# Second mixer: six weight units and the step widths computed from unscaled rows, their outputs multiplied by the token norm's root

## The chip, the core and the metric

One core of a Trainium2 chip runs the whole kernel. Its engines are TensorE (PE, with its weight loads shown apart as PEld), VectorE (DVE), ScalarE (ACT), GpSimd (POOL) and SyncE (SP), which issues the transfers. Each engine takes its own instructions in order, and they meet through semaphores. The metric is device time in microseconds (us) of one execution.

## The reference

The program is two transformer blocks over 256 tokens of width 1024. The first block (a mixer and a mixture of experts, ending in a layer norm) leaves `h`, 256 x 1024. The second block begins with the part that is changed:

```python
u = rmsnorm(h, norm_mix_w)            # h * rsqrt(mean(h*h) + EPS) * w, one root for each token
proj = u @ w_in                       # 1024 x 10272
gate_a, gate_s, b_a, c_a, v_a, z, xbc, dt_raw = split(proj)
y_a = (b_a * causal_dwconv(c_a * v_a)) @ w_a_out
...                                   # scan over xbc with the step widths softplus(dt_raw + dt_bias)
merged = sigmoid(gate_a) * y_a + sigmoid(gate_s) * y_s
h = h + merged @ w_o
```

The root belongs to a token and the sum of `u @ w_in` runs over features, so the root may be applied to the rows before the product or to the product's columns of that token behind it.

## The kernel before

Everything is fp32 in and out. A product of two fp32 matrices is made of three passes in fp32r: each operand is split into a high part (rounded by an ACT copy) and a low part (the rest, by a DVE subtract), and `product3` (L168, L169, L170) issues high x high, low x high and high x low.

The second mixer (`mixer2`) streams 56 weight units. A unit is 1024 x 256 weights (1 MB). SP loads it into one of three slots; ACT makes the high part (`split_hi`, L112, 128x2048), DVE the low part (`split_lo`, L116), and PE multiplies (`unit`, `gemm`, `features_out`: 2 x 8 x 3 matmuls of 128x256), with features on the partitions and the 256 tokens along the free dimension, into one of three banks in turn. The high part of unit n overwrites that of unit n-3, so `split_hi(n)` waits for the end of unit n-3:

```python
def split_hi(act, n):
    st.hi(act, n // 3, n % 3, KD * COLS, n - 2 if n >= 3 else None)
```

Units 0 to 11 hold b_a, c_a and v_a; their outputs are copied by ACT from the bank into `bcv` (`evac`, L1725), each copy ahead of `split_hi(n + 3)` in ACT's order. Units 12 to 23 go through a convolution. Units 0 to 2 are written out in PE's code, units 3 to 23 are a loop.

The start of the mixer runs in this order. DVE finishes the layer norm of the first block for token tile 0, then tile 1 (L228), and each adds one to `s.h_ready`. ACT computes for each tile the mean of squares and the root (L1702, L234, L236) and writes `diag`, the identity times the root (L1706). PE has six filler matmuls (L1993) in front, waits for both tiles, and turns `h` by 16 fp32 matmuls with `diag` on the moving side (L1998), so the rows in banks 3 to 6 are turned and scaled by the root at once. ACT copies them with the norm's weight into `u_hi` (L1709), DVE makes `u_lo` (L1838), and unit 0 starts, its first eight products each waiting for one `u_lo`. Behind unit 0 PE multiplies the 32 columns of the step widths (`w_dt_hi`, `w_dt_lo`), ACT copies the 32 rows out (L1712), PE turns them in two small transposes behind unit 1 (L2022), and DVE and ACT compute softplus (L1844 to L1849, L1715 to L1721).

DVE's own order at that place is `split_lo(0)`, two small operations (`half_norm_w`, `w_dt_lo`), the eight `u_lo`, `split_lo(1)`, `split_lo(2)`, the step widths, and then `split_lo(3)` to `split_lo(14)`.

Of the kernel before, what the change touches and what calls it, by code (L numbers as in the profile page):

```python
# [1552 lines left out]
def mixer2(nc, A, s):  # L1553

    XBC_TAPS, A_TAPS, N_HEADS, N_GROUPS = 4, 3, 32, 4
    with ExitStack() as ctx:
        def sb(name, shape, dt=FP32):
            return ctx.enter_context(nc.sbuf_tensor(name, shape, dt))
# [64 lines left out]
        bank_of, use_of = {}, {}  # L1623
# [71 lines left out]
        def scalar(act):  # L1695
# [1 line left out]
            split_hi(act, 1)  # L1697
            act.wait_ge(par_loaded, 48)
            act.activation(w_dt_hi[:, :, :], w_dt[:, :, :], ACT.Copy).then_inc(w_dt_split, 1)
            for t in range(TT):  # L1700
                act.wait_ge(s.h_ready, t + 1)
                own.add(act.activation(squares_of_h, s.h[:, t, :], ACT.Square, accum_out=mv[:, t, 0:1]))  # L1702
                own.wait()
                inverse_root(act, own, mv[:, t, 2:3], mv[:, t, 1:2], mv[:, t, 0:1], 1.0 / D, s.eps_ln, r_ready)
                act.wait_ge(r_ready, t + 1)
                act.activation(diag[:, t, :], C("identity"), ACT.Copy, scale=mv[:, t, 2:3]).then_inc(diag_ready, 1)  # L1706
            for k in range(KD):
                act.wait_ge(ut_mm, k // 2 + 1)
                act.activation(u_hi[:, k, :], s.bank[3 + k // 2][:, T * (k % 2):T * (k % 2) + T], ACT.Copy, scale=s.col("norm_mix_w_2", k)).then_inc(ut_hi, 1)  # L1709
            split_hi(act, 2)  # L1710
            act.wait_ge(dt_heads_mm, 1)
            act.activation(dt_heads, s.bank[7][0:N_HEADS, P:P + T], ACT.Copy).then_inc(dt_copied, 1)  # L1712
            act.preload_act_table_set(LOG_EXP)
            act.wait_ge(dt_raw, 1)
            own.add(act.activation(dt_tmp[:, :, :], dt[:, :, :], ACT.Abs))  # L1715
# [7 lines left out]
            def evac(n, dst, func, scale=1.0, signal=None):  # L1723
                act.wait_ge(st.gemm_done, n + 1)
                act.activation(dst, s.bank[bank_of[n]][:, :], func, scale=scale).then_inc(signal or evac_sem[bank_of[n]], 1)  # L1725

            for n in range(12):
                evac(n, pair(bcv, n), ACT.Copy)
                split_hi(act, n + 3)

            def ya_part(j):
                act.wait_ge(ya_ready, j + 1)
# [95 lines left out]
        def vector(dve):  # L1828
# [5 lines left out]
            dve.wait_ge(w_dt_split, 1)  # L1834
            dve.tensor_tensor(w_dt_lo[:, :, :], w_dt[:, :, :], w_dt_hi[:, :, :].bitcast(FP32), ALU.subtract).then_inc(w_dt_split, 1)
            for k in range(KD):
                dve.wait_ge(ut_hi, 2 * (k // 2) + 2)
                dve.scalar_tensor_tensor(out=u_lo[:, k, :], in0=s.bank[3 + k // 2][:, T * (k % 2):T * (k % 2) + T], scalar=s.col("norm_mix_w_2", k),  # L1838
                                         in1=u_hi[:, k, :].bitcast(FP32), op0=ALU.mult, op1=ALU.subtract).then_inc(ut_lo, 1)
            for n in range(1, 3):  # L1840
                split_lo(dve, n)
            dve.wait_ge(dt_mm, 1)
            dve.wait_ge(par_loaded, 48)
            dve.tensor_tensor(dt[:, :, :], s.bank[7][:, 0:64].rearrange("p (t h) -> p t h", t=TT),  # L1844
# [3 lines left out]
            dve.wait_ge(dt_ready, 1)  # L1848
            dve.scalar_tensor_tensor(out=loga[:, :, :], in0=dt[:, :, :], scalar=-1.0, in1=a_col[:, :].unsqueeze(1).to_broadcast([P, TT, N_HEADS]),  # L1849
                                     op0=ALU.mult, op1=ALU.mult).then_inc(dt_ready, 1)  # L1850
            for n in range(3, 15):
                split_lo(dve, n)

            def conv_a_part(j):

# [134 lines left out]
        def tensor(pe):  # L1990

            for i in range(6):
                pe.matmul(s.bank[1][:, :], lhsT=C("identity"), rhs=s.con[:, 1:5, :].rearrange("p n c -> p (n c)"), start=True, stop=True)  # L1993
            pe.wait_ge(s.h_ready, 2)
            for t in range(TT):
                pe.wait_ge(diag_ready, t + 1)
                for k in range(KD):
                    m = pe.matmul(s.bank[3 + k // 2][:, T * (k % 2) + P * t:T * (k % 2) + P * t + P], lhsT=s.h[:, t, k * P:k * P + P], rhs=diag[:, t, :], start=True, stop=True)  # L1998
                    if t == 1 and k % 2:
                        m.then_inc(ut_mm, 1)  # L2000

            def gemm(q, i, bank, x, first=True, last=True, used=None, wait_k=None):

# [5 lines left out]
            def unit(n, x, **kw):  # L2009
                gemm(n // 3, n % 3, bank_of[n], x, used=use_of[n], **kw)  # L2010

            u, ya = (u_hi, u_lo), (ya_hi, ya_lo)
            unit(0, u, wait_k=lambda k: pe.wait_ge(ut_lo, k + 1))

            pe.wait_ge(w_dt_split, 2)
            for k in range(KD):
                m = product3(pe, s.bank[7][0:N_HEADS, P:P + T], (w_dt_hi[:, k, :], w_dt_lo[:, k, :]), (u_hi[:, k, :], u_lo[:, k, :]), k == 0, k == KD - 1)
            m.then_inc(dt_heads_mm, 1)
            unit(1, u)
            pe.wait_ge(dt_copied, 1)  # L2020
# [495 lines left out]
```

## Time and profile before

| what | value |
|---|---|
| time, median of 3 runs (lowest to highest) | 1704.86 us (1702.92 to 1706.76) |
| profiled execution: time, span in the trace | 1705.02 us, 1703.2 us |
| granted TensorE clock, mean over the span | 0.995 |
| PE busy | 1655.8 us (97%) |
| DVE busy | 676.8 us (40%) |
| ACT busy | 577.0 us (34%) |
| second mixer's first unit starts, in the trace | 1146.38 us |

The span is the part of the profiled execution that the trace covers; 1.8 us lie around it. A clock of 1.00 is the full 2.4 GHz, 0.50 is 1.2 GHz. Busy matmuls overlap each other in the trace (a 128x256 matmul is shown with 0.28 us, and the next begins 0.12 us after it), so PE's progress is read from starts.

### The profile page before, as it was taken

The page shows a single profiled execution, that of the slowest core. Times are in us where ns is not written, and L with a number is a line of the kernel's source. Part 1 is how long each engine was busy: PE and PEld are TensorE (multiplying, and loading weights), DVE is VectorE, ACT ScalarE, POOL GpSimd, SP SyncE. Part 2 cuts the span into 40 slices and gives each one's busy share as a digit, 9 for nine tenths or more (in the row PEclk, how much of TensorE's full clock was granted, in tenths as well). Part 3 has the DMA queues.
Part 4 walks back from the last instruction along what each step waited for, and adds up shares of the span by engine and source line. Part 5 has one row for each costly group of instructions (what it writes and reads, how often), then busy time and mean ns, then how long its engine had stood idle before and what let it go on. Part 6 is the DMA issues. An engine that isn't in the chain of part 4 may idle for free.

```text
span 1703.2 us, 23986 instructions
## 1 busy us (share of the span) xinstructions
PE 1655.8 (97%) x9921; PEld 1053.1 (62%) x9921; DVE 676.8 (40%) x1196; ACT 577.0 (34%) x819; POOL 42.8 (3%) x28
## 2 busy tenths in 40 slices
PE   8999999989999999999999999989999999999998
PEld 8999853333333333333333333349999999989996
DVE  4676641212121211121212121244597565666654
ACT  5655321111111111110111111144464787466433
POOL 0000000000000000000000000000100032000000
PEclk9999999999999999999999999999999999999999
DMA  8556899999999999999999999975555443555552
GB/s 266 199 198 222 303 392 423 428 412 428 431 430 431 431 428 431 429 431 429 432 429 431 428 429 428 431 279 182 181 179 174 149 149 124 177 182 183 187 185 87
DMA packets 150864, 535.15 MB, mean 314 GB/s; under 512 B 7890, under 2 KB 102510, under 8 KB 118030
## 3 DMA queue, kind: packets, MB, share of 16 engines
q1 hardware_dynamic: 150798, 534.20, 79.7%
q8 instruction: 50, 0.82, 0.2%
q14 instruction: 16, 0.13, 0.0%
HBM read 533.13 MB, written 1.05 MB: 314 GB/s over the span
## 4 chain that ended last, share of the span: by engine, by line
PE 62%; DMA 12%; SPq 2%; ACT 1%; DVE 1%; issue 0%; ACTq 0%
PE bank L1434 16%; PE bank L168 10%; PE bank L170 10%; PE bank L169 10%; PE bank L1450 8%; DMA expert_weights<-in_expert_w_up_dram 6%; DMA expert_weights_late<-in_expert_w_up_dram 6%; PE bank L1395 2%; PE bank L1414 2%; PE bank L1441 2%; SPq L1642 1%; PE bank L1403 1%; PE bank L2046 0%; ACT back_w_hi L112 0%; PE bank L1408 0%
## 5 line engine op out<-in xcount | busy, mean ns | idle before, releaser
L1332 DVE TENSOR_TENSOR pre_act<-bank,bias_now 128x512 f32<-128x512 f32 x64 | 44.0, 688 | 655.3 <-PE bank L1441 655.3
L116 DVE TENSOR_TENSOR back_w_lo<-raw_weights,back_w_hi 128x2048 fp32r<-128x2048 f32 x90 | 205.7, 2288 | 91.8 <-ACT back_w_hi L112 90.8
L1434 PE MATMUL bank<-expert_weights_late,x_gathered 128*64 128x512 f32 x1024 | 226.2, 593 | 13.7 <-DMA expert_weights_late<-in_expert_w_up_dram 13.7
L112 ACT ACTIVATE back_w_hi<-raw_weights 128x2048 fp32r<-128x2048 f32 x90 | 170.2, 1892 | 95.1 <-PE bank L170 94.6
L168 PE MATMUL bank<-u_hi,back_w_hi 128*128 128x256 f32 x704 | 200.0, 284 | 0.2 <-DVE u_lo L1838 0.2
L169 PE MATMUL bank<-u_lo,back_w_hi 128*128 128x256 f32 x704 | 199.1, 283 | 0.0
L170 PE MATMUL bank<-u_hi,back_w_lo 128*128 128x256 f32 x704 | 199.1, 283 | 0.0
L1434 PE MATMUL bank<-expert_weights,x_gathered 128*64 128x512 f32 x752 | 167.0, 594 | 8.7 <-DMA expert_weights<-in_expert_w_up_dram 8.7
L1434 PEld LDWEIGHTS bank<-expert_weights_late,x_gathered 128*64 128x64 f32 x1024 | 72.3, 137 | 164.2 <-issue 136.2
L1254 ACT ACTIVATE raw_weights<-bank 128x512 f32<-128x512 f32 x32 | 19.1, 597 | 399.6 <-PE bank L1434 399.6
L168 PEld LDWEIGHTS bank<-u_hi,back_w_hi 128*128 128x128 f32 x704 | 135.0, 192 | 1.0 <-issue 0.7
L169 PEld LDWEIGHTS bank<-u_lo,back_w_hi 128*128 128x128 f32 x704 | 135.0, 192 | 0.0
L170 PEld LDWEIGHTS bank<-u_hi,back_w_lo 128*128 128x128 f32 x704 | 135.0, 192 | 0.0
L1434 PEld LDWEIGHTS bank<-expert_weights,x_gathered 128*64 128x64 f32 x752 | 53.0, 137 | 118.9 <-issue 99.7
L1450 PE MATMUL bank<-expert_weights_late,activations 128*64 128x512 f32 x512 | 113.4, 595 | 0.2 <-DVE activations L1345 0.2
L168 PE MATMUL bank<-v_hi,back_w_hi 128*128 128x256 f32 x352 | 99.9, 284 | 0.2 <-DVE v_lo L2266 0.2
L169 PE MATMUL bank<-v_lo,back_w_hi 128*128 128x256 f32 x352 | 99.6, 283 | 0.0
L170 PE MATMUL bank<-v_hi,back_w_lo 128*128 128x256 f32 x352 | 99.6, 283 | 0.0
L1270 ACT ACTIVATE raw_weights<-bank 128x512 f32<-128x512 f32 x32 | 19.1, 597 | 206.2 <-PE bank L1450 206.2
L1450 PE MATMUL bank<-expert_weights,activations 128*64 128x512 f32 x368 | 82.0, 594 | 0.0
L168 PE MATMUL bank<-x_hi,m_w_hi 128*128 128x256 f32 x272 | 78.1, 287 | 0.0
L169 PE MATMUL bank<-x_lo,m_w_hi 128*128 128x256 f32 x272 | 76.8, 282 | 0.0
(424 smaller groups left out, 2649.9 us busy)
## 6 DMA issues: line engine op xcount, KB each, us to landing
expert_weights_late<-in_expert_w_up_dram SPq DMA_DIRECT2D x64, 2048.0 KB, 25.6
expert_weights<-in_expert_w_up_dram SPq DMA_DIRECT2D x47, 2048.0 KB, 25.3
expert_weights_late<-in_expert_w_down_dram SPq DMA_DIRECT2D x32, 2048.0 KB, 29.2
raw_weights<-in_w_in_dram SPq DMA_DIRECT2D x56, 1024.0 KB, 5.3
expert_weights<-in_expert_w_down_dram SPq DMA_DIRECT2D x23, 2048.0 KB, 28.6
raw_weights<-in_expert_w_up_dram SPq DMA_DIRECT2D x15, 2048.0 KB, 23.8
raw_weights<-in_w_up_dram SPq DMA_DIRECT2D x22, 1024.0 KB, 5.1
raw_weights<-in_expert_w_down_dram SPq DMA_DIRECT2D x8, 2048.0 KB, 28.7
```

The source lines that it names most:

```text
L112: act.activation(self.w_hi[:, s, 0:size], self.s.raw[:, s, 0:size], ACT.Copy).then_inc(self.hi_done, 1)
L116: dve.tensor_tensor(self.w_lo[:, s, 0:size], self.s.raw[:, s, 0:size], self.w_hi[:, s, 0:size].bitcast(FP32), ALU.subtract).then_inc(self. ...
L168: pe.matmul(out, lhsT=ah, rhs=bh, start=start, stop=False, skip_group_check=shared)
L169: pe.matmul(out, lhsT=ah, rhs=bl, start=False, stop=False, skip_group_check=shared)
L170: return pe.matmul(out, lhsT=al, rhs=bh, start=False, stop=stop, skip_group_check=shared)
L1254: act.activation(up_rows[:, 0, :], U[0][:, :], ACT.Copy).then_inc(up_out, 1)
L1332: dve.tensor_tensor(both.rearrange("p g k n -> p (g k) n").rearrange("p a (h n) -> p a h n", h=2), TB[b][:, :].rearrange("p (a h n) -> p a ...
L1395: m = pe.matmul(TB[0][rows[c], :], lhsT=onehot[:, t, :], rhs=s.h[:, t, 512 * c:512 * c + 512], start=(t == 0), stop=(t == 1))
L1414: m = pe.matmul(s.bank[ACC + 2 * t + c][:, :], lhsT=scatter[rows[c], P * t:P * t + P], rhs=y_rows[rows[c], :], start=False, stop=True, ski ...
L1434: m = pe.matmul(U[b][rows[half], :], lhsT=xg[:, 2 * u + a, :], rhs=w[:, a, 512 * c:512 * c + 512], start=(first and a == 0), stop=(last an ...
L1441: m = pe.transpose(TB[b][:, P * gk:P * gk + P], up_rows[:, b, gk:512:4], C("identity"))
L1450: m = pe.matmul(U[0][rows[c], :], lhsT=act_t[:, b, g, half, :], rhs=w[:, half, g, 512 * c:512 * c + 512], start=(b + half + g == 0), stop= ...
```

## The change

The rows of `h` are now turned without the root, by transposes against the identity. ACT and DVE split them into `raw_u_hi` and `raw_u_lo`, and units 0 to 5 and the step widths are multiplied from these. ACT computes the root of tile 0 ahead of the raw high parts and that of tile 1 behind them. PE spreads the roots over the partitions by two matmuls of a matrix of ones with `diag` (into bank 2), ACT copies them to `root_rows`, and DVE multiplies the outputs of units 0 to 5 (`scaled_copy`, in place of ACT's copies) and the step widths by them. Meanwhile DVE makes the scaled rows `scaled_u` from the turned banks, ACT and DVE split them into `u_hi` and `u_lo`, two rows at a time among the units' own work, and from unit 6 on PE uses `u_hi` and `u_lo` as before. PE waits once for all eight `u_lo`, ahead of unit 6. Units 0 to 5 are written out, units 6 to 23 are the loop.

```diff
@@ scalar (ACT)
-            for t in range(TT):
+            def root(t):
                 act.wait_ge(s.h_ready, t + 1)
 ...
+            root(0)
             for k in range(KD):
                 act.wait_ge(ut_mm, k // 2 + 1)
-                act.activation(u_hi[:, k, :], s.bank[3 + k // 2][:, T * (k % 2):T * (k % 2) + T], ACT.Copy, scale=s.col("norm_mix_w_2", k)).then_inc(ut_hi, 1)
+                act.activation(raw_u_hi[:, k, :], turned(k), ACT.Copy, scale=s.col("norm_mix_w_2", k)).then_inc(raw_hi, 1)
+            root(1)
             split_hi(act, 2)
-            act.wait_ge(dt_heads_mm, 1)
-            act.activation(dt_heads, s.bank[7][0:N_HEADS, P:P + T], ACT.Copy).then_inc(dt_copied, 1)
+            act.wait_ge(bc_mm, 1)
+            act.activation(root_rows, s.bank[2][:, 0:T], ACT.Copy).then_inc(bc_ready, 1)
+            split_hi(act, 3)
 ...
             for n in range(12):
-                evac(n, pair(bcv, n), ACT.Copy)
-                split_hi(act, n + 3)
+                if n >= RAW_UNITS:
+                    evac(n, pair(bcv, n), ACT.Copy)
+                if n:
+                    split_hi(act, n + 3)
+                if 1 <= n < 5:
+                    for k in range(2 * n - 2, 2 * n):
+                        act.wait_ge(rescaled, k + 1)
+                        act.activation(u_hi[:, k, :], scaled_u[:, k, :], ACT.Copy).then_inc(ut_hi, 1)
@@ vector (DVE)
+            dve.wait_ge(bc_ready, 1)
+            dve.wait_ge(dt_heads_mm, 1)
+            dve.tensor_tensor(dt_heads, s.bank[7][0:N_HEADS, P:P + T], root_rows[0:N_HEADS, :], ALU.mult).then_inc(dt_copied, 1)
+
+            def scaled_copy(n):
+                dve.wait_ge(st.gemm_done, n + 1)
+                dve.tensor_tensor(bcv[:, 2 * n:2 * n + 2, :], s.bank[bank_of[n]][:, :].rearrange("p (a t) -> p a t", a=2),
+                                  root_rows.unsqueeze(1).to_broadcast([P, 2, T]), ALU.mult).then_inc(evac_sem[bank_of[n]], 1)
+
+            scaled_copy(0)
+            split_lo(dve, 3)
 ...
-            for n in range(3, 15):
-                split_lo(dve, n)
+            for n in range(1, 12):
+                if n < RAW_UNITS:
+                    scaled_copy(n)
+                if n < 3:
+                    for k in range(4 * n - 4, 4 * n):
+                        dve.scalar_tensor_tensor(out=scaled_u[:, k, :], in0=turned(k), scalar=s.col("norm_mix_w_2", k), in1=root_rows,
+                                                 op0=ALU.mult, op1=ALU.mult).then_inc(rescaled, 1)
+                split_lo(dve, n + 3)
+                if 2 <= n < 6:
+                    for k in range(2 * n - 4, 2 * n - 2):
+                        dve.wait_ge(ut_hi, k + 1)
+                        dve.tensor_tensor(u_lo[:, k, :], scaled_u[:, k, :], u_hi[:, k, :].bitcast(FP32), ALU.subtract).then_inc(ut_lo, 1)
@@ tensor (PE)
+            def turn_u(t, k):
+                return pe.transpose(turned(k)[:, P * t:P * t + P], s.h[:, t, k * P:k * P + P], C("identity"))
+
+            pe.wait_ge(s.h_ready, 1)
+            for k in range(6):
+                turn_u(0, k)
             pe.wait_ge(s.h_ready, 2)
-            for t in range(TT):
-                pe.wait_ge(diag_ready, t + 1)
-                for k in range(KD):
-                    m = pe.matmul(s.bank[3 + k // 2][:, T * (k % 2) + P * t:T * (k % 2) + P * t + P], lhsT=s.h[:, t, k * P:k * P + P], rhs=diag[:, t, :], start=True, stop=True)
-                    if t == 1 and k % 2:
-                        m.then_inc(ut_mm, 1)
+            for k in range(KD):
+                if k >= 6:
+                    turn_u(0, k)
+                m = turn_u(1, k)
+                if k % 2:
+                    m.then_inc(ut_mm, 1)
 ...
-            unit(0, u, wait_k=lambda k: pe.wait_ge(ut_lo, k + 1))
+            unit(0, raw_u, wait_k=lambda k: pe.wait_ge(raw_lo, k + 1))
 ...
+            for t in range(TT):
+                pe.wait_ge(diag_ready, t + 1)
+                m = pe.matmul(s.bank[2][:, P * t:P * t + P], lhsT=C("ones"), rhs=diag[:, t, :], start=True, stop=True)
+            m.then_inc(bc_mm, 1)
+            unit(1, raw_u)
 ...
-            unit(2, u)
-            with pe.Fori(1, 8) as q:
+            pe.wait_ge(bc_ready, 1)
+            for n in range(2, RAW_UNITS):
+                unit(n, raw_u)
+            pe.wait_ge(ut_lo, KD)
+            with pe.Fori(RAW_UNITS // 3, 8) as q:
                 for i in range(3):
                     gemm(q, i, i, u, used=q)
```

Two places in the engines' orders matter. The first is DVE between the layer norm's end and unit 12 (the `x_b_c` row is unit 12's convolution). Before, with `back_w_lo` the weights' low parts:

```order
L228 SCALAR_TENSOR_TENSOR hidden<-hidden,expert_weights_top 128x1024
L116 TENSOR_TENSOR back_w_lo<-raw_weights,back_w_hi 128x2048
L1833 TENSOR_SCALAR half_norm_w<-parameter_cols 128x16
L1835 TENSOR_TENSOR w_dt_lo<-w_dt,w_dt_hi 128x256
L1838 SCALAR_TENSOR_TENSOR u_lo<-bank,parameter_cols,u_hi 128x256 x8
L116 TENSOR_TENSOR back_w_lo<-raw_weights,back_w_hi 128x2048 x2
L1844 TENSOR_TENSOR dt<-bank,dt_bias 128x64
L1847 SCALAR_TENSOR_TENSOR dt<-dt,dt_tmp 128x64
L1849 SCALAR_TENSOR_TENSOR log_a<-dt,a_log 128x64
L116 TENSOR_TENSOR back_w_lo<-raw_weights,back_w_hi 128x2048 x12
```

The same place now, from the low part of weight unit 5 (the `b_c_v` rows are `scaled_copy`, `squares` holds `root_rows`, `gates` holds `scaled_u`, whose eight rows are made further ahead in two groups of four):

```order
L116 TENSOR_TENSOR back_w_lo<-raw_weights,back_w_hi 128x2048
L1890 TENSOR_TENSOR u_lo<-gates,u_hi 128x256 x2
L1865 TENSOR_TENSOR b_c_v<-bank,squares 128x512
L116 TENSOR_TENSOR back_w_lo<-raw_weights,back_w_hi 128x2048
L1890 TENSOR_TENSOR u_lo<-gates,u_hi 128x256 x2
L1865 TENSOR_TENSOR b_c_v<-bank,squares 128x512
L116 TENSOR_TENSOR back_w_lo<-raw_weights,back_w_hi 128x2048
L1890 TENSOR_TENSOR u_lo<-gates,u_hi 128x256 x2
L1865 TENSOR_TENSOR b_c_v<-bank,squares 128x512
L116 TENSOR_TENSOR back_w_lo<-raw_weights,back_w_hi 128x2048
L1890 TENSOR_TENSOR u_lo<-gates,u_hi 128x256 x2
```

The four L116 rows are the low parts of units 5, 6, 7 and 8, and the three L1865 rows between them multiply the outputs of units 3, 4 and 5. So the low part of a weight unit now stands between each two pairs of `u_lo`, and that of unit 8 ahead of the last pair.

The second place is ACT's order from the layer norm's end to the step widths (L112 is the high part of a weight unit). Before, with L1702 to L1706 the root of a tile:

```order
L1702 ACTIVATE z,rms_mv<-hidden 128x1024
L234 ACTIVATE rms_mv<-rms_mv,eps 128x1
L236 ACTIVATE rms_mv<-rms_mv 128x1
L1706 ACTIVATE group_rstd<-shared_constants,rms_mv 128x128
L1702 ACTIVATE z,rms_mv<-hidden 128x1024
L234 ACTIVATE rms_mv<-rms_mv,eps 128x1
L236 ACTIVATE rms_mv<-rms_mv 128x1
L1706 ACTIVATE group_rstd<-shared_constants,rms_mv 128x128
L1709 ACTIVATE u_hi<-bank,parameter_cols 128x256 x8
L112 ACTIVATE back_w_hi<-raw_weights 128x2048
L1712 ACTIVATE z<-bank 32x256
```

Now, with L1709 to L1713 the root and L1722 the copy to `root_rows`:

```order
L1709 ACTIVATE z,rms_mv<-hidden 128x1024
L234 ACTIVATE rms_mv<-rms_mv,eps 128x1
L236 ACTIVATE rms_mv<-rms_mv 128x1
L1713 ACTIVATE group_rstd<-shared_constants,rms_mv 128x128
L1718 ACTIVATE raw_u_hi<-bank,parameter_cols 128x256 x8
L1709 ACTIVATE z,rms_mv<-hidden 128x1024
L234 ACTIVATE rms_mv<-rms_mv,eps 128x1
L236 ACTIVATE rms_mv<-rms_mv 128x1
L1713 ACTIVATE group_rstd<-shared_constants,rms_mv 128x128
L112 ACTIVATE back_w_hi<-raw_weights 128x2048
L1722 ACTIVATE squares<-bank 128x256
L112 ACTIVATE back_w_hi<-raw_weights 128x2048
```

The eight high parts have moved ahead of the second tile's root, and the step widths' copy has become DVE's.

## Rows read from the trace of the kernel before

**Rows 1.** The page, part 4: the chain that ended last, by engine.
```profile
PE 62%; DMA 12%; SPq 2%; ACT 1%; DVE 1%; issue 0%; ACTq 0%
```

**Rows 2.** Windows: length, busy time by engine, clock, DMA share, GB/s.
```profile
1140.50:1146.30 5.80, 5.46 (x32) 5.27 (x32) 3.33 (x6) 3.47 (x9) 0.37 (x2) 0.71 0.37 107
1160.00:1250.00 90.00, 90.00 (x749) 89.65 (x748) 51.87 (x54) 46.90 (x49) 8.42 (x5) 1.00 0.58 176
```

**Rows 3.** The chain in order of time, 1125 to 1250: start, length, what.
```profile
1139.38 1.30 DVE hidden L228
1140.72 4.14 PE bank L1998 x20
```

**Rows 4.** Timeline before unit 0: start, length, engine, line, [idle before <-releaser].
```profile
1133.20 5.42 PE L1993 MATMUL bank<-shared_constants 128*128 128x512 f32 x12
...
1136.74 1.29 DVE L228 SCALAR_TENSOR_TENSOR hidden<-hidden,expert_weights_top 128x1024 f32<-128x1024 f32 x1
...
1140.58 2.29 DVE L116 TENSOR_TENSOR back_w_lo<-raw_weights,back_w_hi 128x2048 fp32r<-128x2048 f32 x1
...
1142.86 0.42 DVE L1835 TENSOR_TENSOR w_dt_lo<-w_dt,w_dt_hi 128x256 fp32r<-128x256 f32 x1
...
1144.88 3.02 ACT L1709 ACTIVATE u_hi<-bank,parameter_cols 128x256 fp32r<-128x256 f32 x8 [2.04 <-PE bank L1998]
1145.75 3.23 DVE L1838 SCALAR_TENSOR_TENSOR u_lo<-bank,parameter_cols,u_hi 128x256 fp32r<-128x256 f32 x8 [2.47 <-ACT u_hi L1709]
...
1146.38 0.36 PE L168 MATMUL bank<-u_hi,back_w_hi 128*128 128x256 f32 x1 [0.20 <-DVE u_lo L1838]
```

**Rows 5.** Timeline: eight fp32 transposes at the program's start.
```profile
5.21 1.06 PE L894 MATMUL bank<-shared_constants,hidden 128*128 128x128 f32 x8 [0.47 <-DMA hidden<-in_x_dram]
```

**Rows 6.** Timeline, PE: start of unit 1, end of unit 2, start of unit 3.
```profile
1155.12 0.28 PE L168 MATMUL bank<-u_hi,back_w_hi 128*128 128x256 f32 x1
...
1166.81 0.28 PE L169 MATMUL bank<-u_lo,back_w_hi 128*128 128x256 f32 x1
1166.93 0.28 PE L170 MATMUL bank<-u_hi,back_w_lo 128*128 128x256 f32 x1
1167.19 0.39 PE L168 MATMUL bank<-u_hi,back_w_hi 128*128 128x256 f32 x1
```

**Rows 7.** Groups by line and shape: xcount | busy us, mean ns | idle before.
```profile
L1998 PE MATMUL bank<-group_rstd,hidden 128*128 128x128 f32 x32 | 5.5, 351 | 2.1 <-DVE hidden L228 2.1
L2318 PE MATMUL bank<-diag,hidden 128*128 128x128 f32 x32 | 3.8, 277 | 1.6 <-ACT diag L2228 1.6
```

**Rows 8.** Timeline of ACT and of DVE around units 3 to 5.
```profile
1167.25 0.60 ACT L1725 ACTIVATE b_c_v<-bank 128x512 f32<-128x512 f32 x1 [0.15 <-PE bank L170]
...
1179.01 0.60 ACT L1725 ACTIVATE b_c_v<-bank 128x512 f32<-128x512 f32 x1 [3.37 <-PE bank L170]
1179.50 1.90 ACT L112 ACTIVATE back_w_hi<-raw_weights 128x2048 fp32r<-128x2048 f32 x1
...
1181.44 2.29 DVE L116 TENSOR_TENSOR back_w_lo<-raw_weights,back_w_hi 128x2048 fp32r<-128x2048 f32 x1 [3.47 <-ACT back_w_hi L112]
```

**Rows 9.** Groups by line and shape: DVE 128x512 from a bank.
```profile
L1907 DVE TENSOR_TENSOR b_c_v<-bank,dt 128x512 f32<-128x512 f32 x8 | 5.0, 684 | 3.3 <-PE bank L2086 3.3
```

**Rows 10.** Windows at the low clock, columns as in group 2.
```profile
1140.98:1144.30 3.32, 3.32 (x17) 3.32 (x17) 2.30 (x3) 1.77 (x5) 0.12 (x2) 0.50 0.11 13
345.70:352.50 6.80, 6.01 (x14) 1.76 (x16) 0.82 (x4) 0.00 (x0) 0.00 (x0) 0.50 1.04 446
```

**Rows 11.** Timeline: PE behind an idle stretch; weight loads as the clock rises.
```profile
346.49 6.61 PE L1434 MATMUL bank<-raw_weights,x_gathered 128*64 128x512 f32 x16 [4.50 <-issue]
...
351.66 0.24 PEld L1434 LDWEIGHTS bank<-raw_weights,x_gathered 128*64 128x64 f32 x2 [0.61 <-issue]
352.50 0.14 PEld L1434 LDWEIGHTS bank<-expert_weights,x_gathered 128*64 128x64 f32 x2 [0.60 <-issue]
352.93 0.14 PEld L1434 LDWEIGHTS bank<-expert_weights,x_gathered 128*64 128x64 f32 x2 [0.29 <-issue]
```

More of the change, by code:

```diff
@@ L1588, in mixer2 @@
         half_w = sb("half_norm_w", [P, 16])
+        RAW_UNITS = 6
+        raw_u_hi, raw_u_lo = sb("raw_u_hi", [P, KD, T], F32R), sb("raw_u_lo", [P, KD, T], F32R)
+        root_rows, scaled_u = squares[1][:, 0:T], gates[:, 0:KD, :]
         C = lambda name: s.con[:, SHARED.index(name), :]
@@ L1605, in mixer2 @@
             "gated", "squared", "ms_mm", "rstd_ready", "normed", "y_hi", "y_done"))
+        raw_hi, raw_lo, bc_mm, bc_ready, rescaled = (sem("m3_" + n) for n in ("raw_hi", "raw_lo", "bc_mm", "bc_ready", "rescaled"))
         w_dt_split, dt_heads_mm, dt_copied = sem("m3_w_dt_split"), sem("m3_dt_heads_mm"), sem("m3_dt_copied")
@@ L1629, in mixer2, with turned @@
             bank_of[n], use_of[n] = bank_of[n + 4], use_of[n + 4]
+        def turned(k):
+            return s.bank[3 + k // 2][:, T * (k % 2):T * (k % 2) + T]
         def split_hi(act, n):
@@ L1836, in vector @@
             for k in range(KD):
-                dve.wait_ge(ut_hi, 2 * (k // 2) + 2)
-                dve.scalar_tensor_tensor(out=u_lo[:, k, :], in0=s.bank[3 + k // 2][:, T * (k % 2):T * (k % 2) + T], scalar=s.col("norm_mix_w_2", k),
-                                         in1=u_hi[:, k, :].bitcast(FP32), op0=ALU.mult, op1=ALU.subtract).then_inc(ut_lo, 1)
+                dve.wait_ge(raw_hi, 2 * (k // 2) + 2)
+                dve.scalar_tensor_tensor(out=raw_u_lo[:, k, :], in0=turned(k), scalar=s.col("norm_mix_w_2", k),
+                                         in1=raw_u_hi[:, k, :].bitcast(FP32), op0=ALU.mult, op1=ALU.subtract).then_inc(raw_lo, 1)
             for n in range(1, 3):
                 split_lo(dve, n)
+            dve.wait_ge(bc_ready, 1)
[7 more added lines that the diff above has]
+            split_lo(dve, 3)
             dve.wait_ge(dt_mm, 1)
@@ L2010, in unit @@
                 gemm(n // 3, n % 3, bank_of[n], x, used=use_of[n], **kw)
-            u, ya = (u_hi, u_lo), (ya_hi, ya_lo)
-            unit(0, u, wait_k=lambda k: pe.wait_ge(ut_lo, k + 1))
+            u, ya, raw_u = (u_hi, u_lo), (ya_hi, ya_lo), (raw_u_hi, raw_u_lo)
+            unit(0, raw_u, wait_k=lambda k: pe.wait_ge(raw_lo, k + 1))
             pe.wait_ge(w_dt_split, 2)
             for k in range(KD):
-                m = product3(pe, s.bank[7][0:N_HEADS, P:P + T], (w_dt_hi[:, k, :], w_dt_lo[:, k, :]), (u_hi[:, k, :], u_lo[:, k, :]), k == 0, k == KD - 1)
+                m = product3(pe, s.bank[7][0:N_HEADS, P:P + T], (w_dt_hi[:, k, :], w_dt_lo[:, k, :]), (raw_u_hi[:, k, :], raw_u_lo[:, k, :]), k == 0, k == KD - 1)
             m.then_inc(dt_heads_mm, 1)
-            unit(1, u)
+            for t in range(TT):
[3 more added lines that the diff above has]
+            unit(1, raw_u)
             pe.wait_ge(dt_copied, 1)
```

## The prediction

> **What bounds the kernel now.** I read the chain that ended last first: PE holds 62% of it [rows 1], so time is won or lost where PE waits or works slower. The windows view then shows where the changed stretch has such places. From 1160 to 1250 us PE is busy in all 90.00 us, so a microsecond by which PE starts units earlier or later goes through to the end: no later wait of PE in this mixer is long enough to swallow it. At the mixer's start, 1140.5 to 1146.3, the granted clock is 0.71 [rows 2]. The chain goes there from DVE's last layer norm row to the turning matmuls L1998 [rows 3], and the timeline gives the rest: the filler matmuls end at 1133.20 + 5.42 = 1138.62, PE waits to 1140.72, ACT's first high part starts at 1144.88, DVE's first low part at 1145.75, unit 0 at 1146.38 [rows 4].
>
> **Front: unit 0 starts earlier.** The turning no longer needs the root or full matmuls. Six transposes can run behind the fillers, since tile 0 is ready at 1136.74 + 1.29 = 1138.03 [rows 4]; eight fp32 transposes take 1.06 us [rows 5]. From 1140.72 the first pair of rows needs two more, so ACT can begin its eight high parts near 1141.1 instead of 1144.88. DVE cannot follow so soon: it is in the low part of weight unit 0 from 1140.58 to 1142.87 and then in `half_norm_w` and `w_dt_lo` until 1142.86 + 0.42 = 1143.28 [rows 4]. Its order there is unchanged, so the first raw low part starts at 1143.28 and not at 1145.75: 2.47 us earlier. The eight low parts pace unit 0's first half (0.40 us each, 3.23 for eight) before and after, and ACT (3.02 for eight) stays ahead. Term: **-2.5 us**. The second root moved behind the high parts costs nothing: it takes some 2 us from 1144.1, and its reader on PE comes after unit 0 and the step widths, more than 8 us after unit 0's start (unit 1 started 1155.12 - 1146.38 = 8.7 us behind it [rows 4, 6]).
>
> **Added on PE.** Two fp32 matmuls of ones with `diag` spread the roots. Sixteen fp32 matmuls of that shape take 3.8 us where the clock is full [rows 7], so two take **+0.5 us** ahead of unit 1. What hides behind PE: the copy of the roots, DVE's product for the step widths and the high and low part of unit 3 all end inside unit 1 and unit 2 (5.8 us each). Unit 3's low part was late before: the last matmul of unit 2 starts at 1166.93 and the first of unit 3 at 1167.19, 0.26 apart where it is 0.12 inside a unit [rows 6]. Now it stands ahead of the softplus: **-0.1 us**.
>
> **Evacuation by DVE.** Six outputs go through DVE instead of ACT: 684 ns each by the nearest row, a 128x512 product from a bank [rows 9]. Added to it are eight `scaled_u`, eight `u_lo` (0.4 us each, L1838 and L1835 [rows 4]) and the step widths. A unit gives DVE 5.8 us and takes 2.29 for its low part; the fullest one adds 0.7 + 1.6 + 0.8. It fits, and no unit from 1 to 5 waits for it. Without that cover (a unit's DVE work over 5.8) each would cost PE the excess.
>
> **The new wait ahead of unit 6.** Here I follow the semaphores. PE waits ahead of unit 6 for all eight `u_lo`. DVE makes the last two behind the low part of weight unit 8 (its order in the change). That low part waits for ACT's high part of unit 8, which overwrites unit 5's slot and so waits until PE has finished unit 5. PE thus waits for a chain that begins at its own last matmul before the wait; nothing covers it. Length: PE's last matmul of a unit ends at about 1166.93 + 0.28 = 1167.21 and ACT starts at 1167.25 [rows 6, 8]; PE's next matmul would have started 0.12 after the last one's start, at 1167.05, so 0.2 us. Between 1179.01, where ACT is released, and 1181.44 + 2.29 = 1183.73, where the low part is done, lie 4.72 us, of which 1179.50 - 1179.01 = 0.49 is the copy that ACT no longer makes [rows 8]: 4.23. `scaled_copy(5)` lies beside ACT's 1.9. Two `u_lo` by L1835 are 0.8, and from DVE's end (1145.75 + 0.48 by the pace of L1838) to PE's start at 1146.38 it is 0.15 [rows 4]. Sum 5.4, less 0.15 as DVE's neighbours overlap: **+5.2 us**. Behind DVE's last two `u_lo` only units 9 and on are queued; the parts of 6, 7 and 8 are ready, so the wait is paid once.
>
> **TensorE's clock at that wait.** The trace has two idle stretches with a fall. After 2.10 us the clock stood at 0.50 (1.2 GHz) from 1140.98 to 1144.30 [rows 4, 10]; the same sixteen matmuls took 5.5 us there and 3.8 at full clock [rows 7], so 1.7 us were lost. After 4.50 us idle it stood at 0.50 from 345.70 to 352.50, 6.01 us of it busy [rows 10, 11]; two rows of weight loads are 0.84 us apart there (351.66 and 352.50) and 0.43 behind it (352.93) [rows 11], so half of 6.01, 3.0 us, was lost. The new wait is longer than both, and nearest to the second, but where in the wait the clock falls moves the loss: in the second it fell 0.8 us before PE began again, and may fall earlier or later here. I take the middle of the two, **+2.4 us**, with 1.7 and 3.0 as ends. The Trainium skill ("TensorE: Matmul & The Clock Gate", Terms) prices low time by the share of pulses withheld, half of it: by that the two stretches cost 1.7 and 3.4, as the second counts 0.8 us in which PE had nothing to do, and the term would be 2.5 and the sum 0.1 us higher. By the rows only low time in which PE works costs anything.
>
> **The clock at the front.** PE now works in short pieces there: transposes near 1138.6 to 1139.5 and 1140.7 to 1142, then idle until 1143.9. Before, one idle stretch of 2.1 us was enough for a fall. Bounds: nothing, if the transposes keep the clock up or it is back by then, and 1.7 us by L1998's row, if unit 0 starts at 1.2 GHz. I take **+1.0 us**.
>
> **Sum**, against the profiled execution's own 1705.0: 1705.0 - 2.5 + 0.5 - 0.1 + 5.2 + 2.4 + 1.0 = 1711.5. That execution is 0.2 us above the median of the three runs, so 1711.3 is the prediction, 6.4 us (0.4%) slower.
>
> **Rivals.** (A) The wait is there and the clock costs nothing at either place: -2.5 + 0.5 - 0.1 + 5.2 = +3.1, 1708.0. For it: PE idled 1.6 us ahead of L2318 and that group still ran at 277 ns [rows 7]. Against it: after 2.1 and 4.5 us idle the clock did fall. (B) Not slower: the last two `u_lo` are ready when unit 5 ends, and PE finds no wait. Then -2.1 and up to 1.0 of clock at the front: 1702.8 to 1703.8. It decides at one point, whether DVE's low part of unit 8 can start before unit 5 has ended. For it: DVE is idle some 3.5 us per unit [rows 8], so the work would fit. Against it: DVE keeps its order, and slot and semaphore tie unit 8 to unit 5. (C) The front's gain does not come: raw high or low parts are held up (for instance by PSUM traffic of both engines), and only the new costs stay: +9, 1714.
>
> **How the numbers follow.** Forecast 0.78, A 0.09, B 0.08, C 0.05. The forecast's own range, with both clock terms at their ends, is +4.8 (1709.7) to +7.8 (1712.7). Reaching down toward A and up by some spread of the runs (1702.92 to 1706.76), the range is 1707.5 to 1713.5. A measurement of this kernel can tell about 0.2%, 3.4 us. The forecast lies above it; A is just inside, B inside on the other side (even with 2.5 us gained the front alone would not pass it). Slower 0.81, same 0.15, faster 0.04.
>
> **What would show it.** Right: unit 0's first matmul 3.2 us (not 5.7) behind the end of the last layer norm row, which was 1139.38 + 1.30 [rows 3], released by DVE and not by ACT; PE idle some 5 us between units 5 and 6, released by a `u_lo` of L1890, with ACT's L112 and DVE's L116 in that gap; a granted clock of 0.50 for some microseconds around unit 6; no idle time at units 1 to 5. Wrong: a gap at unit 6 under 1 us (then B), a full clock at unit 6 (then A), or unit 0 no earlier (then C).

## The result and the profile after

The changed kernel takes 1710.81 us (median of 6 runs, 1709.93 to 1711.28) where the kernel before took 1704.51 us beside it (6 runs, 1702.92 to 1706.76). The ratio is 1.0044, 95% interval 1.0034 to 1.0053: slower by 6.3 us. The forecast was 1711.3, in 1707.5 to 1713.5. The profiled execution has a span of 1709.1 us.

The view of waits of the changed kernel, PE alone, from 1125 to 1230 us (waiting line <- releaser: us in total, times, longest):

```profile
PE bank L168 <- DVE u_lo L1890: 5.4, 1, 5.4
PE bank L168 <- DVE raw_u_lo L1855: 1.8, 1, 1.8
PE bank L2033 <- DVE hidden L228: 1.4, 1, 1.4
PE bank L1414 <- ACT raw_weights L1270: 0.7, 1, 0.7
```

The first is new and long: it is the wait ahead of unit 6. The next two are PE's short idle stretches at the front, in place of the one of 2.1 us [rows 7]. The last lies ahead of the front, in the first block, which the change leaves as it was. The front in the timeline of the changed kernel, which answers to [rows 4] (L2033 are the transposes, L1718 the raw high parts, L1855 the raw low parts):

```profile
1138.22 0.82 PE L2033 MATMUL bank<-shared_constants,hidden 128*128 128x128 f32 x6
...
1139.14 1.28 DVE L228 SCALAR_TENSOR_TENSOR hidden<-hidden,expert_weights_top 128x1024 f32<-128x1024 f32 x1
...
1140.34 2.29 DVE L116 TENSOR_TENSOR back_w_lo<-raw_weights,back_w_hi 128x2048 fp32r<-128x2048 f32 x1
1140.48 1.31 PE L2033 MATMUL bank<-shared_constants,hidden 128*128 128x128 f32 x10 [1.44 <-DVE hidden L228]
...
1140.95 3.03 ACT L1718 ACTIVATE raw_u_hi<-bank,parameter_cols 128x256 fp32r<-128x256 f32 x8 [0.70 <-PE bank L2033]
...
1142.95 3.22 DVE L1855 SCALAR_TENSOR_TENSOR raw_u_lo<-bank,parameter_cols,raw_u_hi 128x256 fp32r<-128x256 f32 x8
1143.58 0.36 PE L168 MATMUL bank<-raw_u_hi,back_w_hi 128*128 128x256 f32 x1 [1.79 <-DVE raw_u_lo L1855]
```

The whole trace lies 0.24 us earlier here, so times are read from the end of the second layer norm row (1139.14 + 1.28 = 1140.42; before, 1139.38 + 1.28 = 1140.66). Unit 0 starts 3.16 us behind it instead of 5.72. ACT begins 0.5 us after the first of the ten transposes; DVE's raw low parts have no idle time ahead of them, so it is DVE's own queue that they wait for.

The gap at unit 6, from the timelines of ACT, DVE and PE of the changed kernel (one fence, three engines; L1865 is `scaled_copy(5)`, L112 and L116 the high and low part of weight unit 8, L1890 the last two `u_lo`):

```profile
1183.28 0.28 PE L170 MATMUL bank<-raw_u_hi,back_w_lo 128*128 128x256 f32 x1
...
1183.60 0.69 DVE L1865 TENSOR_TENSOR b_c_v<-bank,squares 128x512 f32<-128x512 f32 x1 [0.79 <-PE bank L170]
1183.65 1.91 ACT L112 ACTIVATE back_w_hi<-raw_weights 128x2048 fp32r<-128x2048 f32 x1 [3.23 <-PE bank L170]
1185.60 2.29 DVE L116 TENSOR_TENSOR back_w_lo<-raw_weights,back_w_hi 128x2048 fp32r<-128x2048 f32 x1 [1.31 <-ACT back_w_hi L112]
1187.81 0.75 DVE L1890 TENSOR_TENSOR u_lo<-gates,u_hi 128x256 fp32r<-128x256 f32 x2
1188.91 0.55 PE L168 MATMUL bank<-u_hi,back_w_hi 128*128 128x256 f32 x1 [5.36 <-DVE u_lo L1890]
```

Read it downward: PE's last matmul of unit 5 ends at 1183.56, ACT starts 0.09 later, DVE's low part 0.04 behind ACT's end, the `u_lo` behind that, and PE 0.35 after DVE. The next matmul would have started at 1183.40 (0.12 after the last start), so the wait costs 1188.91 - 1183.40 = 5.5 us.

Windows of the changed kernel (columns as in [rows 2]): the two stretches at the low clock, and the part of the second in which PE works:

```profile
1144.76:1148.17 3.41, 3.41 (x18) 3.41 (x17) 3.41 (x5) 2.96 (x6) 0.00 (x0) 0.50 0.77 267
1185.80:1192.50 6.70, 3.58 (x17) 3.62 (x18) 2.76 (x3) 0.00 (x0) 0.00 (x0) 0.50 0.66 203
1188.90:1192.50 3.60, 3.58 (x17) 3.60 (x18) 0.00 (x0) 0.00 (x0) 0.00 (x0) 0.50 0.97 288
```

At the front the clock fell 1.2 us after unit 0 had started (1143.58); at the wait it fell in the idle time, and only 3.6 of the 6.7 us hit work. DVE's added groups, by line and shape, 1140 to 1190 (xcount | busy us, mean ns | idle before):

```profile
L1865 DVE TENSOR_TENSOR b_c_v<-bank,squares 128x512 f32<-128x512 f32 x6 | 4.1, 684 | 2.1 <-PE bank L170 2.1
L1884 DVE SCALAR_TENSOR_TENSOR gates<-bank,parameter_cols,squares 128x256 f32<-128x256 f32 x8 | 3.3, 474 | 0.0
L1890 DVE TENSOR_TENSOR u_lo<-gates,u_hi 128x256 fp32r<-128x256 f32 x8 | 3.0, 417 | 0.0
```

684 ns is what L1907 took before [rows 9]. The outputs' products wait for PE, not PE for them.

From the timelines I took four marks of every run, each from the end of the second L228 row: unit 0's first matmul, the length of unit 0 (to the first `w_dt_hi` matmul), unit 1's first matmul, and ACT's first row of unit 12 (`x_b_c` from a bank). From the last mark to the end of the span it is 478.0 to 478.1 us in all ten runs, so what the change does is over by unit 12. The rows from which the second and the last mark are read, of the kernel before and then of the changed kernel:

```profile
1152.38 0.28 PE L168 MATMUL bank<-u_hi,w_dt_hi 128*32 128x256 f32 x1
1225.09 1.02 ACT L1740 ACTIVATE x_b_c<-bank,parameter_cols 128x256 f32<-128x256 f32 x2 [3.36 <-PE bank L170]
```
```profile
1150.94 0.28 PE L168 MATMUL bank<-raw_u_hi,w_dt_hi 128*32 128x256 f32 x1
1231.10 1.02 ACT L1757 ACTIVATE x_b_c<-bank,parameter_cols 128x256 f32<-128x256 f32 x2 [3.36 <-PE bank L170]
```

| run | unit 0 starts | unit 0 takes | unit 1 starts | unit 12 |
|---|---|---|---|---|
| before | 5.72 | 6.00 | 14.46 | 84.43 |
| changed | 3.16 | 7.36 | 13.68 | 90.68 |
| e1_ulo_first | 3.16 | 7.28 | 13.61 | 83.42 |
| e2_ulo_mid | 3.16 | 5.99 | 12.32 | 85.62 |
| e3_raw9 | 3.16 | 5.98 | 12.31 | 82.12 |
| e4_warm_wait | 3.16 | 7.32 | 13.64 | 89.04 |
| e5_warm_front | 3.16 | 5.99 | 12.32 | 90.29 |
| e6_first_warm | 3.16 | 5.99 | 12.32 | 82.14 |
| e7_first_warm_small | 2.74 | 5.98 | 11.89 | 81.71 |
| e8_before_warm | 4.49 | 5.97 | 13.20 | 83.17 |

The changed kernel's 90.68 - 84.43 = 6.25 us fits the measured 6.3. The marks are those of one profiled execution of each kernel.

### The profile page after: what moved, and what is told of

It reads as the page before. It is cut to its first block, busy times and chain, and to the rows that moved or that the text cites. A ratio compares the mean times of both kernels' runs of the same rounds, so it can differ in the third digit from the quotient of the medians.

```text
span 1709.1 us, 23983 instructions
## 1 busy us (share of the span) xinstructions
PE 1654.7 (97%) x9909; PEld 1052.6 (62%) x9909; DVE 686.6 (40%) x1219; ACT 576.4 (34%) x821; POOL 42.8 (3%) x28
## 4 chain that ended last, share of the span: by engine, by line
PE 62%; DMA 14%; DVE 2%; ACT 1%; issue 0%; SPq 0%; ACTq 0%
PE bank L1434 16%; PE bank L168 10%; PE bank L170 10%; PE bank L169 10%; PE bank L1450 9%; DMA expert_weights_late<-in_expert_w_up_dram 8%; DMA expert_weights<-in_expert_w_up_dram 6%; PE bank L1414 2%; PE bank L1395 2%; PE bank L1441 2%; PE bank L1403 1%; DVE back_w_lo L116 1%; PE bank L2097 0%; ACT back_w_hi L112 0%; PE bank L1408 0%
## 5 line engine op out<-in xcount | busy, mean ns | idle before, releaser
L116 DVE TENSOR_TENSOR back_w_lo<-raw_weights,back_w_hi 128x2048 fp32r<-128x2048 f32 x90 | 205.7, 2287 | 90.8 <-ACT back_w_hi L112 89.8
L112 ACT ACTIVATE back_w_hi<-raw_weights 128x2048 fp32r<-128x2048 f32 x90 | 170.1, 1891 | 107.6 <-PE bank L170 106.7
L168 PE MATMUL bank<-u_hi,back_w_hi 128*128 128x256 f32 x608 | 173.3, 285 | 5.4 <-DVE u_lo L1890 5.4
L169 PE MATMUL bank<-u_lo,back_w_hi 128*128 128x256 f32 x608 | 172.7, 284 | 0.0
L170 PE MATMUL bank<-u_hi,back_w_lo 128*128 128x256 f32 x608 | 172.7, 284 | 0.0
L168 PEld LDWEIGHTS bank<-u_hi,back_w_hi 128*128 128x128 f32 x608 | 117.4, 193 | 5.9 <-DVE back_w_lo L116 5.5
L169 PEld LDWEIGHTS bank<-u_lo,back_w_hi 128*128 128x128 f32 x608 | 117.5, 193 | 0.0
L170 PEld LDWEIGHTS bank<-u_hi,back_w_lo 128*128 128x128 f32 x608 | 117.4, 193 | 0.0
```

Of the source, the lines that this page charges most:

```text
L112: act.activation(self.w_hi[:, s, 0:size], self.s.raw[:, s, 0:size], ACT.Copy).then_inc(self.hi_done, 1)
L116: dve.tensor_tensor(self.w_lo[:, s, 0:size], self.s.raw[:, s, 0:size], self.w_hi[:, s, 0:size].bitcast(FP32), ALU.subtract).then_inc(self. ...
```

## The experiments

The first four ran on one chip and the last four on another, each beside the kernel before, whose median was 1702.46 us on the first and 1702.86 on the second. So ratios are compared, and marks of the table above. The changed kernel itself was not run beside them; experiments 4 and 5, which keep its wait, came out at 1.0032 and 1.0029 there. The theory: the loss is PE's wait ahead of unit 6 with the low clock behind it, against a gain at the front. The main rival: it is the work added on DVE and PE.

**1. The u_lo pairs first in DVE's loop** (e1_ulo_first). Lines are only moved:

```diff
             for n in range(1, 12):
+                if 2 <= n < 6:
+                    for k in range(2 * n - 4, 2 * n - 2):
+                        ...u_lo...
                 if n < RAW_UNITS:
                     scaled_copy(n)
 ...
                 split_lo(dve, n + 3)
-                if 2 <= n < 6:
-                    for k in range(2 * n - 4, 2 * n - 2):
-                        ...u_lo...
```

> Only DVE's order in its loop changes: each pair of u_lo stands ahead of the product of the units' outputs and of the weights' low part, so the last pair is ready before unit 5 ends. Theory (the wait ahead of unit 6 and the clock behind it are the loss): PE's idle 5.4 us there is gone, unit 6 runs at full clock, time 1710.8 - 5.4 - 1.9 = 1703.5, a little faster than before's 1704.5. Rival 1 (the loss comes from the work added on DVE and PE): nothing is taken away, 1710 to 1711. Rival 2 (the idle time goes elsewhere, to a later unit): the gap moves and the time stays above 1708.

Measured: 1702.09 us, ratio 0.9999 (0.9990 to 1.0008). PE's waits in the same stretch, and DVE's timeline around the end of unit 5 (L1883 is now the `u_lo` line):

```profile
PE bank L168 <- DVE raw_u_lo L1855: 1.8, 1, 1.8
PE bank L2033 <- DVE hidden L228: 1.4, 1, 1.4
PE bank L1414 <- ACT raw_weights L1270: 0.7, 1, 0.7
```
```profile
1179.08 0.75 DVE L1883 TENSOR_TENSOR u_lo<-gates,u_hi 128x256 fp32r<-128x256 f32 x2
1180.62 0.69 DVE L1865 TENSOR_TENSOR b_c_v<-bank,squares 128x512 f32<-128x512 f32 x1 [0.79 <-PE bank L170]
1182.62 2.29 DVE L116 TENSOR_TENSOR back_w_lo<-raw_weights,back_w_hi 128x2048 fp32r<-128x2048 f32 x1 [1.32 <-ACT back_w_hi L112]
```

The wait of 5.4 us is gone and nothing has taken its place; the last pair is ready at 1179.83, 0.8 us before DVE sees unit 5's end. All the same work is done, so the rival falls: the order of two lines makes the difference between 1.0044 and 0.9999. It does not become faster than before. The low clock at the front (unit 0 in 7.28 us) accounts for that only in this profile, since experiment 3 has the same ratio with unit 0 in 5.98. Executions with the same granted clock over the whole span do differ: at 0.997 the four of this experiment average 1700.8 us and the ten of the kernel before 1702.5, at 0.996 two average 1702.2 and seven 1704.1. But 6 of the 11 executions here had 0.996 or less, and 10 of the 28 of the kernel before. So the front's gain is there, and a lower clock in more of the executions takes it back; in which stretch, the executions without a profile do not show.

**2. The pairs between product and low part** (e2_ulo_mid). The same lines, behind `scaled_copy(n)` and ahead of `split_lo(n + 3)`.

> As the one before, but each pair of u_lo stands between the product of the unit's output and the weights' low part: the wait ahead of unit 6 then holds one product (0.7) and two u_lo (0.75) and the hand-overs (0.35), 1.8 us. Theory (the wait's length sets the loss): idle 1.8 us instead of 5.4; the clock stays full behind so short a gap (it stayed full ahead of L2318 after 1.6 us) or costs up to 1.9: 1705.3, at most 1707.2. Rival 1 (added work): 1710 to 1711.

Measured: 1704.26 us, ratio 1.0012 (1.0003 to 1.0021), between the two others. The timeline of PE at unit 6 and half-microsecond windows behind it:

```profile
1184.06 0.36 PE L168 MATMUL bank<-u_hi,back_w_hi 128*128 128x256 f32 x1 [1.75 <-DVE u_lo L1889]
```
```profile
1184.50:1185.00 0.50, 0.50 (x7) 0.50 (x6) 0.50 (x1) 0.00 (x0) 0.00 (x0) 1.00 1.09 389
1185.00:1185.50 0.50, 0.50 (x6) 0.50 (x5) 0.50 (x1) 0.00 (x0) 0.00 (x0) 0.63 0.81 277
1188.00:1188.50 0.50, 0.50 (x5) 0.50 (x4) 0.00 (x0) 0.00 (x0) 0.00 (x0) 0.50 0.86 150
1188.50:1189.00 0.50, 0.50 (x6) 0.50 (x6) 0.00 (x0) 0.00 (x0) 0.00 (x0) 0.96 0.85 242
```

The wait is 1.75 us as expected. The hope that the clock stays up behind so short a gap failed: it fell some 1.1 us after PE had resumed (0.63 in the second window) and stayed low to about 1188.5 (0.96 in the last). Against the third experiment, whose front is the same, the mark at unit 12 is 85.62 - 82.12 = 3.5 later: 1.9 of wait (idle 1.75 and the tail of the last matmul, 0.16) and 1.6 of clock.

**3. Nine units unscaled** (e3_raw9).

```diff
-        RAW_UNITS = 6
+        RAW_UNITS = 9
```

> One number changes: nine units instead of six use the unscaled rows, so DVE multiplies nine outputs and PE waits for u_lo ahead of unit 9. Theory (the wait): the last u_lo come 3 units before they are wanted, no gap at unit 9 nor at unit 6, 1703.5. Rival 1 (work added on DVE is what costs): three more products of 0.7 us, so 1710.8 or up to 1713.

Measured: 1702.41 us, ratio 0.9999 (0.9990 to 1.0008). PE's waits:

```profile
PE bank L168 <- DVE raw_u_lo L1855: 1.8, 1, 1.8
PE bank L2033 <- DVE hidden L228: 1.4, 1, 1.4
PE bank L1414 <- ACT raw_weights L1270: 0.7, 1, 0.7
```

DVE does three products more than in the changed kernel and the time falls by as much as in the first experiment. So DVE's work is not what costs, and the place of PE's wait relative to the last `u_lo` is.

**4. Fillers in the wait** (e4_warm_wait).

```diff
+            for i in range(5):
+                pe.matmul(s.bank[7][:, :], lhsT=C("identity"), rhs=s.con[:, 1:5, :].rearrange("p n c -> p (n c)"), start=True, stop=True)
             pe.wait_ge(ut_lo, KD)
```

> Five filler matmuls of 128x512 fp32 (0.9 us each) into an unused bank ahead of the wait for u_lo: the wait stays, TensorE works in it. Theory (about 1.9 us of the loss is the low clock in unit 6): granted clock 1.00 through unit 6, unit 6 in 5.8 instead of 7.6 us, time 1710.8 - 1.9 = 1708.9. Rival (the clock's term is small, or the fall has another cause than the idle): 1710.8, unit 6 still 7.6 us.

Measured: 1707.65 us, ratio 1.0032 (1.0020 to 1.0045), against 1.0044 of the changed kernel. Timeline of PE, and windows over the gap and unit 6:

```profile
1183.97 4.45 PE L2076 MATMUL bank<-shared_constants 128*128 128x512 f32 x10
1189.48 0.36 PE L168 MATMUL bank<-u_hi,back_w_hi 128*128 128x256 f32 x1 [1.06 <-DVE u_lo L1890]
```
```profile
1183.00:1190.00 7.00, 5.94 (x24) 3.22 (x23) 4.04 (x6) 1.91 (x1) 0.00 (x0) 1.00 0.56 159
1190.00:1196.00 6.00, 6.00 (x52) 6.00 (x51) 0.00 (x0) 0.49 (x1) 0.00 (x0) 1.00 0.50 164
```

Unit 6 starts as late as in the changed kernel (5.5 us), but at full clock. The mark at unit 12 comes 90.68 - 89.04 = 1.6 us earlier with the same front (unit 0 in 7.32 and 7.36). So of the loss at unit 6, 1.6 us are clock and 5.5 are wait. The times alone do not separate this from the rival, whose 1.0044 lies within the interval; the clock and the marks do.

**5. Fillers at the front** (e5_warm_front), in the changed kernel, into bank 1, which unit 1 uses first:

```diff
             for k in range(6):
                 turn_u(0, k)
+            for i in range(1):
+                pe.matmul(s.bank[1][:, :], lhsT=C("identity"), rhs=s.con[:, 1:5, :].rearrange("p n c -> p (n c)"), start=True, stop=True)
             pe.wait_ge(s.h_ready, 2)
 ...
                     m.then_inc(ut_mm, 1)
+            for i in range(2):
+                pe.matmul(s.bank[1][:, :], lhsT=C("identity"), rhs=s.con[:, 1:5, :].rearrange("p n c -> p (n c)"), start=True, stop=True)
```

> The changed kernel with three filler matmuls of 128x512 fp32 among the transposes at the front (one behind the six of tile 0, two behind the last), in TensorE's idle stretches there. Theory (unit 0 ran at the low clock in the changed kernel's profile and paid 1.4 us for it): no low clock between 1136 and 1150, unit 0 in 6.0 instead of 7.4 us, ratio to before 1.0044 - 0.0008 = 1.0036. Rival (the fillers delay the transposes or unit 0): unit 0 starts later than 1143.6, ratio 1.0044 or more.

Measured: 1707.66 us, ratio 1.0029 (1.0017 to 1.0041). Windows over the front with unit 0, and over the low stretch at unit 6:

```profile
1136.00:1150.00 14.00, 13.02 (x92) 10.71 (x91) 12.36 (x16) 9.44 (x21) 0.37 (x2) 1.00 0.43 131
1184.00:1191.20 7.20, 5.83 (x27) 5.86 (x28) 1.02 (x3) 0.00 (x0) 0.00 (x0) 0.53 0.49 146
```

Unit 0 starts at the same mark and takes 5.99 us at full clock, 1.4 us less than in the changed kernel's profile. By time, its interval overlaps the changed kernel's (1.0034 to 1.0053). At unit 6 the same wait cost more clock this time: 5.83 us of work lay in the low stretch instead of 3.58. The mark at unit 12 gives 90.29 - 82.14 = 8.15 against the next experiment, whose front is the same; less 5.5 of wait, 2.65 of clock.

**6. Both: pairs first, fillers at the front** (e6_first_warm).

> The first experiment's order (u_lo ahead, no wait at unit 6) and the fillers at the front. Theory: what is left is the front's gain of 2.5 us less 0.4 for the roots' matmuls, with no clock term: 2.1 us faster than before, ratio 0.9988. Rival (the front gains nothing that lasts; the first experiment's 0.9999 is all there is): 0.9999.

Measured: 1701.20 us, ratio 0.9991 (0.9982 to 1.0000). Windows over the front and over units 5 to 7:

```profile
1136.00:1150.00 14.00, 13.35 (x83) 10.10 (x82) 13.93 (x18) 10.20 (x21) 0.37 (x2) 1.00 0.39 117
1178.00:1192.00 14.00, 14.00 (x119) 14.00 (x118) 7.96 (x6) 4.94 (x6) 0.00 (x0) 1.00 0.59 181
```

No low clock and no idle PE at units 5 to 7. The mark at unit 12 is 84.43 - 82.14 = 2.3 us earlier than before; by time 0.9991 fits the theory's 0.9988, and the interval does not exclude the rival's 0.9999.

**7. DVE's small operations behind the raw low parts** (e7_first_warm_small). In addition `half_norm_w` and `w_dt_lo` move behind the eight `raw_u_lo`.

> As the one before, and DVE's two small operations (half_norm_w, w_dt_lo) stand behind the eight raw low parts. Theory (DVE's order ahead of the raw low parts sets unit 0's start, not the transposes nor ACT): unit 0 0.4 us earlier, released by DVE still, ratio 0.9986. Rival (PE or ACT sets it): unit 0 starts where it did.

Measured: 1700.53 us, ratio 0.9987 (0.9978 to 0.9996), the fastest, and clear of no change. Timeline of its front:

```profile
1138.52 2.28 DVE L116 TENSOR_TENSOR back_w_lo<-raw_weights,back_w_hi 128x2048 fp32r<-128x2048 f32 x1
...
1139.13 3.02 ACT L1718 ACTIVATE raw_u_hi<-bank,parameter_cols 128x256 fp32r<-128x256 f32 x8
...
1140.72 1.65 DVE L1852 SCALAR_TENSOR_TENSOR raw_u_lo<-bank,parameter_cols,raw_u_hi 128x256 fp32r<-128x256 f32 x4
...
1141.34 0.46 PE L168 MATMUL bank<-raw_u_hi,back_w_hi 128*128 128x256 f32 x1
```

The raw low parts follow the split of unit 0 at once, and unit 0 starts 2.74 us behind the layer norm instead of 3.16: the 0.42 of the moved operations. So DVE's order sets the front, as the prediction had it. (PE, busy with fillers, is not shown as waiting.)

**8. The kernel before with two fillers in its idle stretch** (e8_before_warm).

```diff
+            for i in range(2):
+                pe.matmul(s.bank[1][:, :], lhsT=C("identity"), rhs=s.con[:, 1:5, :].rearrange("p n c -> p (n c)"), start=True, stop=True)
             pe.wait_ge(s.h_ready, 2)
             for t in range(TT):
                 pe.wait_ge(diag_ready, t + 1)
```

> The kernel before with two filler matmuls of 128x512 fp32 (0.9 us each) in TensorE's 2.1 us of idle ahead of the turning matmuls L1998, nothing else. Theory (the low clock cost the kernel before 1.7 us in L1998, and the change gave that back with the rest of the front): L1998 in 3.8 instead of 5.5 us, unit 0 up to 1 us earlier (two of three low-clock microseconds lie ahead of ACT's first copy), ratio 0.9992 to 0.9994. Rival (L1998's length does not set unit 0's start): ratio 1.0000.

Measured: 1703.22 us, ratio 0.9998 (0.9989 to 1.0007): by time inconclusive, since both expectations lie in the interval. Its timeline (L2000 is L1998 moved down):

```profile
1138.77 4.23 PE L2000 MATMUL bank<-group_rstd,hidden 128*128 128x128 f32 x32 [0.38 <-DVE hidden L228]
...
1140.94 1.86 PEld L2000 LDWEIGHTS bank<-group_rstd,hidden 128*128 128x128 f32 x16 [0.31 <-ACT group_rstd L1706]
...
1141.69 3.03 ACT L1709 ACTIVATE u_hi<-bank,parameter_cols 128x256 fp32r<-128x256 f32 x8 [0.80 <-PE bank L2000]
```

In the profiled execution the sixteen matmuls took 4.23 us instead of 5.46 [rows 2], and unit 0 started 5.72 - 4.49 = 1.2 us earlier. They did not reach the expected 3.8, because the second tile's half now waited for ACT's second root (the PEld row). So in the profiled executions about half of the front's 2.56 us was the low clock in the kernel before, which is absent here without the change; that the time gains by it is not shown.

## Why the prediction was right

The forecast was the likeliest case, slower through a wait ahead of unit 6, and it held in its mechanism and nearly in each term. Before and changed, from the marks and the timeline:

| term | predicted, us | measured, us | from |
|---|---|---|---|
| unit 0 earlier | -2.5 | -2.6 | 3.16 - 5.72 |
| clock at the front | +1.0 | +1.4 | unit 0 in 7.36, not 6.00 |
| roots' matmuls | +0.5 | +0.4 | unit 1: 13.68 - 14.46, less the two above |
| unit 3 not late | -0.1 | -0.2 | remainder to 6.25 |
| wait at unit 6 | +5.2 | +5.5 | 1188.91 - 1183.40 |
| clock at unit 6 | +2.4 | +1.7 | remainder behind the wait against e3 |
| sum | +6.5 | +6.25 | unit 12: 90.68 - 84.43 |

The wait is the cause: shown by taking it away in two ways with all the work kept (experiments 1 and 3) and by shortening it (2). Its length was a little undersized: 0.35 us lie between DVE's last end and PE's start, where I took 0.15 from the front (0.36 in experiment 2 and 0.35 in 4, both at full clock).

The clock term at unit 6 was shown apart from the wait (4), and was oversized for that execution: 1.7 here, 2.65 in experiment 5. I had taken the middle of 1.7 and 3.0 from two stretches, and the two executions of the same wait lie on both sides of it. The price by the Trainium skill ("TensorE: Matmul & The Clock Gate", Terms), half of the low time, gives an estimate of 3.35 for the 6.7 us here; 1.7 were paid, since PE was idle in 3.1 of them. In experiment 2, where PE worked in all of the low time (about 3.4 us), half of it and the measured 1.6 agree.

The front: DVE's order paced it (7), and the second root behind the high parts cost nothing: PE did not wait for `diag`. The -2.5 us hold against an execution of the kernel before with the low clock in L1998, as the one that they were read from; against experiment 8, which ran L1998 at full clock, unit 0 is 4.49 - 3.16 = 1.3 us earlier. The clock there was the term with the widest bounds, 0 to 1.7, and it came out at nothing or near the upper end: in the five profiles with the same front (changed, e1 to e4) unit 0 took 7.36, 7.28, 5.99, 5.98 and 7.32 us. The two clock terms missed by +0.4 and -0.7 and nearly cancelled, so that the sum came within 0.3 us is in part luck.

Of the rivals, A (no clock cost) fell with the low stretch at unit 6, B (no wait) with the 5.4 us in the view of waits, C (no gain at the front) with 3.16 against 5.72. The evacuation by DVE cost nothing, as said: its products wait for PE, and three more of them (3) changed nothing.

One thing the prediction did not see: the loss was avoidable within the change. The pairs of `u_lo` were ready to be made earlier, so the version with them ahead, TensorE kept at work at the front and DVE's two small operations moved back is faster than both kernels: 0.9987 of the kernel before (7).

## What to carry to other kernels

When a new wait is put ahead of a unit, follow what stands ahead of the awaited instruction on its own engine, and whether any of that is released by the waiting engine itself: here the low part of unit 8, which needed the slot of the unit just finished, stood ahead of the last two `u_lo`, and nothing hid it. Moving work "into the gaps" of a loop puts it behind the loop's own waits, so what another engine needs soonest goes ahead of the iteration's first wait. An idle TensorE can cost twice, once in time and once in clock (5.5 and 1.7 us here), and the second is seen only in the granted clock of the stretch in which it works again.

## What the runs showed of the hardware that was not expected

A gap of 1.75 us in TensorE's work cost as much clock (1.6 us) as one of 5.4 us in the changed kernel (1.7 us). The clock fell some 1.1 us after work had resumed in the first case and 3.1 us before it in the second. And the same code at the front ran unit 0 at full clock in two profiled executions (experiments 2 and 3) and partly at 1.2 GHz in three, a difference of 1.3 us that comes and goes with nothing changed there. With fillers in the idle stretches the clock was full at the front in all four profiles (experiments 5 to 8). A single profile's low-clock term should therefore be carried as a range.
